# Two regroupings in a 14-stage transformer kernel: value products among the heads, and turned copies ahead of other work

## The chip, the cores and the metric

The kernel runs on one core of one Trainium2 chip. The time is the device time of one execution in microseconds (us), the median of the runs shown. A core has a matrix engine (TensorE, called PE in the rows; its weight loads are PEld), VectorE (DVE), ScalarE (ACT), GpSimd (POOL) and SyncE (SP), which issues most of the DMAs. The engines run their own lists of instructions in program order and wait for one another by counting semaphores.

## The reference, cut to what matters

Two transformer blocks run one after the other on 512 tokens of width 1024; the weights are float32. The change touches the hybrid mixer of the first block, the key and value products of the memory (256 rows) for its cross attention, and the sparse attention of the second block.

```python
def hybrid_mixer(hn, ...):
    z = hn @ w_in
    y_a = gmlp_spatial_gating(za[..., :D_A], za[..., D_A:], ln_a_g, ln_a_b, w_s, b_s)
    y_b = conformer_conv(zb[..., :D_B], zb[..., D_B:], conv_b_w, conv_b_b, gn_b_g, gn_b_b)
    y_c = mlstm_group(...)                       # 4 heads of 128
    return jnp.concatenate([y_a, y_b, y_c], axis=-1) @ w_out

def cross_attention(hn, mn, w_xq, w_xkv, w_xo):
    kv = mn @ w_xkv                              # mn = rmsnorm(mem): 256 x 1024
    k = kv[..., :D_MODEL].reshape(Bsz, M, N_XHEADS, DH_X)
    v = kv[..., D_MODEL:].reshape(Bsz, M, N_XHEADS, DH_X)
...
# second block, sparse attention, for each block of queries:
        p_s = masked_softmax(s_s, (kpos <= t[:, None])[:, :, None])
        o_s = jnp.einsum('bghqn,bgqnd->bghqd', p_s.astype(v_sel.dtype), v_sel)
```

## The kernel before, in words

**Number format.** Every float32 matrix product is made of three products: a rounded high part and the rest of each operand are held apart (`x_hi`, `x_lo`, `w_hi`, `w_lo`), and `hi*hi`, `hi*lo`, `lo*hi` are added up in PSUM. Small products (the gates, the heads, the attention) use plain float32.

**Weight tiles.** All weights come as one stream of 309 tiles of 128x1024, in the order in which `weight_stream` writes them, through a ring of four slots. SP loads tile t into `raw` when tile t-4 has been split. POOL splits it (L2389 writes `w_hi`, L2391 writes `w_lo`), and may start when PE has finished tile t-4 (`tile_done`). PE waits for `weights_split`, and for `tile_out`, which counts results taken out of PSUM by ACT or DVE. Tiles 0 to 16 are the mixer's input product, 17 to 32 the memory's keys and values (`mem_kv`: eight key tiles, then eight value tiles), 33 to 40 the mixer's output product (`mix_out`).

**PSUM.** There are eight banks of 512 columns: `acc` 0 to 3 and `misc` 0 to 3.

**The mixer on PE.** After the input product PE runs, by hand-written order: `cell_in(0)` (projections of head 0), `mem_k(0)` (one key tile: 24 products of 256 columns), `conv_mean` (two means of the convolution branch), `gating` (two products of the spatial gate, L651 and L655), `cell_scores(0)`, `mem_k(1)`, `cell_out(0)`. Then each of heads 1 to 3 is `cell_in`, `mem_k`, `cell_scores`, `mem_k`, `cell_turn` (transposes of the head before), `cell_out`. Then come the eight value tiles `mem_v(half, j)`: each half of the value's columns takes four tiles, 12 products of 512 columns each, into `acc` 0 and 1, and the second half waits until ACT has drained the first. `conv_var` and `cell_turn(3)` lie between them. Then `opening_of` runs the first three tiles of `mix_out` chunk by chunk (72 products of 512 columns), each chunk when ACT has written `y_hi` and DVE `y_lo` for it. `y_hi` and `y_lo` share memory with `mn_hi` and `mn_lo`, the normed memory, so ACT writes no `y_hi` until all of `mem_kv` is done.

**What the gate waits for.** `gating` needs `v_tok`, the normed tokens of the gate: DVE centres the convolution branch (L1896, which needs `conv_mean`), then does L1901, L1906 and L1909, four operations of 128x256 each. `cell_out(0)` waits for DVE's products of the gate (L1916).

**The memory norm.** Its sum of squares is one PE product after the first opening; ACT and DVE then write `mn_hi` and `mn_lo` chunk by chunk (`rms_high`, `rms`). DVE's convolution of the mLSTM branch (L1834, L1835) starts when five input tiles are out.

**Sparse attention.** There are 14 batches b. For each, PE makes scores (`n_scores`, L910, L914), DVE takes the maximum (`n_max`, L2207), ACT the exponential (`n_exp`, L1484), DVE the scaling (`n_scale`, L2217 to L2222). PE turns the probabilities (`n_turn`, L926) into `misc` 0 and 1; ACT copies the one to `pt_n` (L1515), DVE the other (L2246); PE multiplies them by the values (`n_values`, L941, L947). Scores run three batches ahead, values one behind.

## Time and profile before

| | before |
|---|---|
| median of 3 runs | 1947.76 us (1945.41 to 1947.98) |
| profiled execution | 1947.59 us, its span 1945.8 us |
| PE busy | 1892.9 us (97%) |
| DVE, ACT, POOL busy | 793.7, 432.0, 1071.2 us |
| mean granted TensorE clock | 0.991 |
| products on PE | 8938 |

The span runs from the first to the last instruction; 1.8 us of the profiled execution lie outside it. Matmuls overlap in the records, so the distance from one start to the next is the cost of a product, not its duration. A granted clock of 1.00 is TensorE's upper level of 2.4 GHz, and 0.50 is its lower level of 1.2 GHz.

### The profile page before, as it was taken

The page shows a single profiled execution, that of the slowest core. Times are in us where ns is not written, and L with a number is a line of the kernel's source. Part 1 is how long each engine was busy: PE and PEld are TensorE (multiplying, and loading weights), DVE is VectorE, ACT ScalarE, POOL GpSimd, SP SyncE. Part 2 cuts the span into 40 slices and gives each one's busy share as a digit, 9 for nine tenths or more (in the row PEclk, how much of TensorE's full clock was granted, in tenths as well). Part 3 has the DMA queues.
Part 4 walks back from the last instruction along what each step waited for, and adds up shares of the span by engine and source line. Part 5 has one row for each costly group of instructions (what it writes and reads, how often), then busy time and mean ns, then how long its engine had stood idle before and what let it go on. Part 6 is the DMA issues. An engine that isn't in the chain of part 4 may idle for free.

```text
span 1945.8 us, 24354 instructions
## 1 busy us (share of the span) xinstructions
PE 1892.9 (97%) x8938; PEld 1516.6 (78%) x8938; DVE 793.7 (41%) x1305; ACT 432.0 (22%) x850; POOL 1071.2 (55%) x622
## 2 busy tenths in 40 slices
PE   7989999999999999999999999999999999999997
PEld 5868787888888888875778888887776778888885
DVE  4965333343342434579451212136523371212126
ACT  4323322310000121045140101023414140101022
POOL 5734663565757656430456665564752446666552
PEclk9989999999999999999999999999999999999998
DMA  5322332222333325210123332222321223332321
GB/s 220 109 65 74 96 102 65 78 96 87 119 98 108 98 84 208 67 55 2 56 76 107 98 97 87 87 95 79 108 87 42 67 75 99 106 99 97 97 87 44
DMA packets 46879, 175.99 MB, mean 90 GB/s; under 512 B 5200, under 2 KB 5328, under 8 KB 46032
## 3 DMA queue, kind: packets, MB, share of 16 engines
q1 hardware_dynamic: 46512, 169.55, 27.0%
q10 hardware_dynamic: 288, 5.31, 0.7%
q8 instruction: 59, 0.97, 0.2%
q14 instruction: 20, 0.16, 0.0%
HBM read 172.74 MB, written 2.10 MB: 90 GB/s over the span
## 4 chain that ended last, share of the span: by engine, by line
PE 94%; DVE 3%; ACT 1%; issue 1%; POOL 0%; DMA 0%; SPq 0%; DVEq 0%; POOLq 0%
PE acc L471 17%; PE acc L473 17%; PE acc L472 17%; PE acc L498 7%; PE acc L494 7%; PE acc L495 7%; PE acc L521 1%; PE acc L522 1%; PE acc L523 1%; PE acc L1052 1%; PE misc L926 1%; PE acc L1054 1%; PE acc L1053 1%; PE acc L542 1%; PE acc L541 1%; PE acc L540 1%
## 5 line engine op out<-in xcount | busy, mean ns | idle before, releaser
L2389 POOL TENSOR_SCALAR w_hi<-raw 128x1024 fp32r<-128x1024 f32 x309 | 331.3, 1072 | 816.8 <-PE acc L498 323.3
L2391 POOL TENSOR_TENSOR w_lo<-raw,w_hi 128x1024 fp32r<-128x1024 f32 x309 | 744.7, 2410 | 25.8
L471 PE MATMUL acc<-x_hi,w_hi 128*128 128x512 f32 x872 | 343.3, 394 | 0.0
L473 PE MATMUL acc<-x_hi,w_lo 128*128 128x512 f32 x872 | 339.6, 389 | 0.0
L472 PE MATMUL acc<-x_lo,w_hi 128*128 128x512 f32 x872 | 339.4, 389 | 0.0
L1790 DVE TENSOR_TENSOR h<-acc,h 128x512 f32<-128x512 f32 x120 | 82.9, 691 | 367.7 <-PE acc L473 234.1
L471 PE MATMUL acc<-y_hi,w_hi 128*128 128x512 f32 x590 | 231.1, 392 | 0.0
L473 PE MATMUL acc<-y_hi,w_lo 128*128 128x512 f32 x590 | 229.6, 389 | 0.0
L472 PE MATMUL acc<-y_lo,w_hi 128*128 128x512 f32 x590 | 229.6, 389 | 0.0
L471 PEld LDWEIGHTS acc<-x_hi,w_hi 128*128 128x128 f32 x872 | 163.8, 188 | 35.4 <-issue 2.3
L473 PEld LDWEIGHTS acc<-x_hi,w_lo 128*128 128x128 f32 x872 | 163.7, 188 | 34.2
L472 PEld LDWEIGHTS acc<-x_lo,w_hi 128*128 128x128 f32 x872 | 163.9, 188 | 32.4
L1530 ACT ACTIVATE z<-acc 128x512 f32<-128x512 f32 x64 | 38.2, 598 | 463.0 <-PE acc L498 351.8
L494 PE MATMUL acc<-y_hi,w_hi 128*128 128x512 f32 x330 | 129.8, 393 | 4.2 <-ACT y_hi L1390 2.9
L2266 DVE TENSOR_TENSOR acc<-acc,z 128x512 f32<-128x512 f32 x64 | 44.6, 697 | 213.0 <-ACT z L1530 213.0
L472 PEld LDWEIGHTS acc<-y_lo,w_hi 128*128 128x128 f32 x590 | 110.7, 188 | 23.9 <-issue 1.0
L471 PEld LDWEIGHTS acc<-y_hi,w_hi 128*128 128x128 f32 x590 | 110.7, 188 | 23.8 <-issue 1.0
L495 PE MATMUL acc<-y_hi,w_lo 128*128 128x512 f32 x330 | 129.0, 391 | 0.0
L473 PEld LDWEIGHTS acc<-y_hi,w_lo 128*128 128x128 f32 x590 | 110.8, 188 | 22.9
L494 PE MATMUL acc<-x_hi,w_hi 128*128 128x512 f32 x240 | 93.7, 391 | 4.5 <-POOL w_lo L2391 2.7
L498 PE MATMUL acc<-y_lo,w_hi 128*128 128x512 f32 x330 | 93.5, 392 | 1.4 <-DVE y_lo L2372 1.4
L495 PE MATMUL acc<-x_hi,w_lo 128*128 128x512 f32 x240 | 93.4, 389 | 0.0
(398 smaller groups left out, 2650.2 us busy)
## 6 DMA issues: line engine op xcount, KB each, us to landing
raw<-weights_dram SPq DMA_DIRECT2D x309, 512.0 KB, 3.5
w_cmp<-w_cmp_dram ACTq DMA_DIRECT2D x1, 4096.0 KB, 14.7
h<-x_dram SPq DMA_DIRECT2D x2, 1024.0 KB, 6.5
out_dram<-h SPq DMA_DIRECT2D x8, 256.0 KB, 2.0
small<-small_dram SPq DMA_DIRECT2D x1, 1408.0 KB, 16.4
small<-small_dram ACTq DMA_DIRECT2D x1, 1088.0 KB, 5.0
mem_in<-mem_dram SPq DMA_DIRECT2D x1, 1024.0 KB, 13.5
const<-const_dram SPq DMA_DIRECT2D x1, 640.0 KB, 9.5
```

The costliest lines, as they stand in the source:

```text
L471: mm(out, m["w_hi"][:, slot, k], hi[:, k], start=k == 0, stop=False)
L472: mm(out, m["w_hi"][:, slot, k], lo[:, k], start=False, stop=False)
L473: last = mm(out, m["w_lo"][:, slot, k], hi[:, k], start=False, stop=k == kc - 1)
L494: mm(acc[:, slot], m["w_hi"][:, slot, k], hi[:, k], start=k == 0, stop=False)
L495: mm(acc[:, slot], m["w_lo"][:, slot, k], hi[:, k], start=False, stop=False)
L498: last = mm(acc[:, slot], m["w_hi"][:, slot, k], lo[:, k], start=False, stop=k == kc - 1)
L521: mm(out, hi[:, k, blk(b)], w_hi[:, blk(i, width)], start=k == 0 and first, stop=False)
L1530: f(z[:, slot], acc[:, slot], ACT.Relu).then_inc(sem(name + "_relu"), 1)
L1790: v.tensor_tensor(h[:, c], acc[:, slot], h[:, c], ALU.add).then_inc(sem("tile_out"), 1)
L2266: v.tensor_tensor(acc[:, slot], acc[:, slot], z[:, slot], ALU.mult).then_inc(sem(name + "_product"), 1)
L2389: nc.gpsimd.tensor_scalar(hi, m["raw"][:, slot], 1.0, 0.0, ALU.mult, ALU.add).then_inc(sem("weights_high"), 1)
L2391: nc.gpsimd.tensor_tensor(m["w_lo"][:, slot].rearrange("p k n -> p (k n)"), m["raw"][:, slot], bf(hi), ALU.subtract).then_inc(sem("weights ...
```

## The change

The change has six parts.

- **Value tiles in quarters.** The eight value tiles now hold 256 columns each, two tiles to a quarter of the columns, and stand in the weight stream between the key tiles (`K_TILE`, `V_TILE`). A tile is 24 products of 256 columns. `mem_v(0)`, `mem_v(1)`, `mem_v(2)` run after `cell_out` of heads 0, 1, 2; five remain after head 3. Quarters 0 and 1 use bank `acc` 1, quarter 2 `acc` 0, quarter 3 `misc` 0, so no drain lies between them at the end. `cell_turn` always uses `acc` 3, and `cell_in` of heads 2 and 3 waits for `cell_y`.
- **Gate products amid the first head.** `conv_mean` runs before `mem_k(0)`, and `cell_scores(0)` before `gating`. On DVE the gate's two products lie between the operations of head 0.
- **First two chunks of the output product apart.** The gate's result has its own `ya_hi` and `ya_lo`, which can be written before `mem_kv` ends; `mix_out` reads them for chunks 0 and 1. The opening no longer waits for all of `mem_kv` to be drained, only for 12 of its 16 results.
- **Memory norm sooner.** PE's sum of squares lies inside the first opening, before chunk 6. ACT writes four chunks of `mn_hi` before and four after the first three input results.
- **mLSTM convolution in pairs.** Its first two channels start when three input results are out.
- **Sparse attention.** In batch 0 ACT and DVE copy the turned probabilities before `n_exp(2)`, and before `n_max(2)` and `pool_low(1)`. On PE `n_values(0)` comes before `n_scores(4)`.

```diff
@@ -64,6 +64,13 @@
 HALF = KC // 2
 
 
+K_TILE = [0, 1, 3, 4, 6, 7, 9, 10]
+V_TILE = [2, 5, 8, 11, 12, 13, 14, 15]
+
+K_OUT = [1, 2, 3, 4, 7, 8, 9, 10]
+V_OUT = [6, 12, 14, 16]
+
...
@@ -337,6 +348,8 @@
                  ("v_stats", [TB, 6]), ("v_mv", [TB, 2]), ("v_rstd", [TB]), ("g_col", [TB, 4]), ("em_col", [TB, 4]),
                  ("cell_r", [TB]), ("cell_s", [TB])])
     assert e <= end, (e, end)
+    place("ya_hi", [2, S], F32R, e - 4 * (TB * 256 + 2 * S + 2 * (CONV_B - 1) + TB * 6 + TB * 2 + 3 * TB + 2 * TB * 4))
+    place("ya_lo", [2, S], F32R, e - 4 * (TB * 256 + TB * 6 + TB * 2 + 3 * TB + 2 * TB * 4))
...
+            if free is None:
+                claim(t0 + j)
+            else:
+                pe.wait_ge(sem("weights_split"), t0 + j + 1)
+                pe.wait_ge(sem("tile_out"), free)
         for k in range(kc):
             if also:
...
+    def memory_norm(k):
+        if k == 6:
+            pe.wait_ge(sem("norm_rstd"), 1)
+            sum_squares("mem", MEM)
+
+    opening(0, 0, "mix", memory_norm)
...
-        t = START["mem_kv"] + c
+        t = START["mem_kv"] + K_TILE[c]
         pe.wait_ge(sem("weights_split"), t + 1)
-        pe.wait_ge(sem("tile_out"), t)
+        pe.wait_ge(sem("tile_out"), START["mem_kv"] + (K_OUT[c - 1] if c else 0))
...
-    def mem_v(half, j):
-
-        t = START["mem_kv"] + 8 + 4 * half + j
+    def mem_v(j):
+
+        t = START["mem_kv"] + V_TILE[j]
         pe.wait_ge(sem("weights_split"), t + 1)
-        if j == 0:
-            pe.wait_ge(sem("tile_out"), t)
...
+        if j == 2:
+            pe.wait_ge(sem("tile_out"), START["mem_kv"] + V_OUT[0])
+        if j == 4:
+            pe.wait_ge(sem("tile_out"), START["mem_kv"] + K_OUT[7])
+        if j == 6:
+            pe.wait_ge(sem("std_scaled"), 1)
+        bank = pr.values_bank(j // 2)
...
+            out = bank[:, blk(b, 256)]
+            for i in range(4):
+                k = 4 * (j % 2) + i
+                w_hi, w_lo = (m[w][:, t % RING].rearrange("p k n -> p (k n)")[:, blk(i, 256)] for w in ("w_hi", "w_lo"))
+                mm(out, m["mn_hi"][:, k, blk(b)], w_hi, start=k == 0 and b == 0, stop=False)
+                mm(out, m["mn_hi"][:, k, blk(b)], w_lo, start=False, stop=False)
+                last = mm(out, m["mn_lo"][:, k, blk(b)], w_hi, start=False, stop=k == KC - 1 and b == 1)
...
+        if head >= 2:
+            pe.wait_ge(sem("cell_y"), head - 1)
...
-            last = turn(acc[:, 1 if head < 3 else 3, blk(tb)], m["cell_tok"][:, tb], ident)
+            last = turn(acc[:, 3, blk(tb)], m["cell_tok"][:, tb], ident)
...
     pe.wait_ge(sem("tile_out"), START["mem_kv"])
     pe.wait_ge(sem("row_cols_out"), 2)
     cell_in(0)
+    for c in range(2):
+        conv_mean(c)
     pe.wait_ge(sem("norm_ready"), chunks_before("mem") + KC)
     mem_k(0)
-    for c in range(2):
-        conv_mean(c)
+    cell_scores(0)
     for c in range(2):
         gating(c)
-    cell_scores(0)
     mem_k(1)
     cell_out(0)
+    mem_v(0)
     for head in range(1, 4):
...
         cell_turn(head - 1)
         cell_out(head)
-    mem_v(0, 0)
-    mem_v(0, 1)
+        if head < 3:
+            mem_v(head)
+    mem_v(3)
+    mem_v(4)
     for c in range(2):
         conv_var(c)
-    mem_v(0, 2)
+    mem_v(5)
     cell_turn(3)
-    mem_v(0, 3)
-    for j in range(4):
-        mem_v(1, j)
+    mem_v(6)
+    mem_v(7)
     pe.wait_ge(sem("cell_y"), 4)
-    pe.wait_ge(sem("tile_out"), END["mem_kv"])
-
-
-    opening_of(START["mix_out"], START["mix_out"], y_hi, y_lo, "y_high", "y_ready", 0)
+
+
+    mix_hi, mix_lo = Parts(m["ya_hi"], 2, y_hi), Parts(m["ya_lo"], 2, y_lo)
+    opening_of(START["mix_out"], START["mix_out"], mix_hi, mix_lo, "y_high", "y_ready", 0, free=START["mem_kv"] + 12)
     for c in range(3, KC):
-        dense(START["mix_out"] + c, (START["mix_out"] + c) % RING, y_hi, y_lo)
+        dense(START["mix_out"] + c, (START["mix_out"] + c) % RING, mix_hi, mix_lo)
...
     for b in range(len(BATCHES)):
         n_turn(b)
+        if b == 1:
+            n_values(0)
         if b + 3 < len(BATCHES):
             n_scores(b + 3)
-        if b:
+        if b > 1:
             n_values(b - 1)
...
+    rms_high("mem", m["mn_hi"], MEM, range(4))
...
-    rms_high("mem", m["mn_hi"], MEM)
...
+    rms_high("mem", m["mn_hi"], MEM, range(4, KC))
...
+        out(START["mem_kv"] + K_TILE[c], 0, m["mem_k"][:, c], src=acc[:, 0, 0:MEM])
+
+    def mem_v(quarter):
+        act.wait_ge(sem("tile_done"), START["mem_kv"] + V_TILE[2 * quarter + 1] + 1)
+        f(m["mem_v"][:, :, blk(quarter, 256)], pr.values_bank(quarter).rearrange("p (b n) -> p b n", b=2), ACT.Copy)\
+            .then_inc(sem("tile_out"), 2)
...
+        if head == 1:
+            mem_v(0)
     cell_root(3)
+    act.wait_ge(sem("y_a"), 2)
+    for c in range(2):
+        f(m["ya_hi"][:, c], m["y_mix"][:, c], ACT.Copy).then_inc(sem("y_high"), 1)
     for c in range(2):
...
         rsqrt(misc[:, c, :], misc[:, c, :], 1.0, LN_EPS, "std_rstd")
+    mem_v(1)
     cell_gain(3)
-    mem_v(0)
     for c in range(2):
         act.wait_ge(sem("std_scaled"), c + 1)
         f(m["conv_b"][:, c], m["conv_b"][:, c], ACT.Silu, scale=pr.col("gn_b_g", c), bias=pr.col("gn_b_b", c))\
             .then_inc(sem("y_b"), 1)
-    mem_v(1)
     act.wait_ge(sem("tile_done"), END["mem_kv"])
-    act.wait_ge(sem("y_a"), 2)
     act.wait_ge(sem("y_b"), 2)
-    for c in range(KC):
+    for c in range(2, KC):
         if c >= 4:
             act.wait_ge(sem("cell_y"), c - 3)
         f(m["y_hi"][:, c], m["y_mix"][:, c], ACT.Copy).then_inc(sem("y_high"), 1)
+    mem_v(2)
+    mem_v(3)
 
     residual_rms("xat", START["mix_out"], "norm_x_g")
 
...
         tb, br, c0, heads = BATCHES[b]
         n = heads * (tb + 1) * P
-        if b + 2 < len(BATCHES):
+        if b and b + 2 < len(BATCHES):
             n_exp(b + 2)
         act.wait_ge(sem("n_turned"), 2 * b + 1)
         if b >= 2:
             act.wait_ge(sem("n_values"), b - 1)
         f(m["pt_n"][:, b % 2, 0, 0:n], misc[:, 0, 0:n], ACT.Copy).then_inc(sem("n_pt0"), 1)
+        if b == 0:
+            n_exp(2)
         if b and BATCHES[b - 1][0] < tb:
             n_high(tb - 1)
     for g in (2, 3):
...
-    dve.wait_ge(sem("tile_out"), 5)
     dve.wait_ge(sem("norm_high"), 2 * KC)
...
+    for pair in range(2):
+        dve.wait_ge(sem("tile_out"), 3 + 2 * pair)
+        before = own.n
...
-    dve.wait_ge(sem("tile_out"), START["mem_kv"])
-    for c in range(2):
+    def gate(c):
         dve.wait_ge(sem("gating"), c + 1)
         v.tensor_tensor(m["u_a"][:, c], m["u_a"][:, c], misc[:, 2 + c, :], ALU.mult).then_inc(sem("y_a"), 1)
...
         v.tensor_tensor(m["y_mix"][:, 4 + head], bank, m["oc_gate"][:, head], ALU.mult).then_inc(sem("cell_y"), 1)
 
     cell_diagonal(0)
+    dve.wait_ge(sem("tile_out"), START["mem_kv"])
+    gate(0)
     cell_weights(0)
+    gate(1)
     cell_norm(0)
     for head in range(1, 4):
         cell_weights(head)
         cell_final(head - 1)
         cell_norm(head)
     for c in range(2):
+        dve.wait_ge(sem("y_high"), c + 1)
+        v.tensor_tensor(m["ya_lo"][:, c], m["y_mix"][:, c], bf(m["ya_hi"][:, c]), ALU.subtract).then_inc(sem("y_ready"), 1)
+    for c in range(2):
         dve.wait_ge(sem("std_rstd"), c + 1)
         v.tensor_tensor(m["conv_b"][:, c], m["conv_b"][:, c], misc[:, c, :], ALU.mult).then_inc(sem("std_scaled"), 1)
     cell_final(3)
-    for c in range(KC):
+    for c in range(2, KC):
...
     v.tensor_copy(m["pct"][:, 4:8], misc[:, 2, :].rearrange("p (j n) -> p j n", j=4)).then_inc(sem("cmp_pt"), 1)
     n_scale(1)
-    n_max(2)
-    pool_low(1)
     pool_order = [(g, k) for g in (2, 3) for k in range(g + 4)]
     for b in range(len(BATCHES)):
         tb, br, c0, heads = BATCHES[b]
@@ -2244,7 +2304,10 @@
         if b >= 2:
             dve.wait_ge(sem("n_values"), b - 1)
         v.tensor_copy(m["pt_n"][:, b % 2, 1, 0:n], misc[:, 1, 0:n]).then_inc(sem("n_pt1"), 1)
-        if 0 < b < len(BATCHES) - 1:
+        if b == 0:
+            n_max(2)
+            pool_low(1)
+        elif b < len(BATCHES) - 1:
             n_scale(b + 1)
         if b + 3 < len(BATCHES):
             n_max(b + 3)

```

The same pattern (chunks 0 and 1 apart, four channels as two pairs) repeats in the lines left out; `Parts` is a small class that picks `ya` for chunks 0 and 1 and `y` for the rest, and `values_bank` holds the banks named above.

On PE around the gate, before; `y_mix,const` is `conv_mean`, `small_64` rows that write `misc` are `gating`, `q_c,k_c` rows are `cell_scores(0)`, `mn` rows belong to a key tile:

```order
L619 MATMUL acc<-mn_hi,w_lo 128x256
L641 MATMUL misc<-y_mix,const 128x512 x2
L651 MATMUL misc<-small_64,const 128x512
L655 MATMUL misc<-small_64,v_tok 64x128 x8
L651 MATMUL misc<-small_64,const 128x512
L655 MATMUL misc<-small_64,v_tok 64x128 x8
L677 MATMUL misc<-q_c,k_c 128x512
L677 MATMUL misc<-q_c,k_c 128x384
L677 MATMUL misc<-q_c,k_c 128x128
L677 MATMUL acc<-q_c,k_c 128x256
L617 MATMUL acc<-mn_hi,w_hi 128x256
```

The same place now, first the start and then the end of the key tile of 24 products:

```order
L710 MATMUL acc<-small_64,xc 128x128 x4
L680 MATMUL misc<-y_mix,const 128x512 x2
L652 MATMUL acc<-mn_hi,w_hi 128x256
L653 MATMUL acc<-mn_lo,w_hi 128x256
L654 MATMUL acc<-mn_hi,w_lo 128x256
```

```order
L654 MATMUL acc<-mn_hi,w_lo 128x256
L718 MATMUL misc<-q_c,k_c 128x512
L718 MATMUL misc<-q_c,k_c 128x384
L718 MATMUL misc<-q_c,k_c 128x128
L718 MATMUL acc<-q_c,k_c 128x256
L690 MATMUL misc<-small_64,const 128x512
L694 MATMUL misc<-small_64,v_tok 64x128 x8
L690 MATMUL misc<-small_64,const 128x512
L694 MATMUL misc<-small_64,v_tok 64x128 x8
L652 MATMUL acc<-mn_hi,w_hi 128x256
```

The means moved ahead of the key tile, and key tile and scores now both lie between them and the gate.

On ACT at the end of the mixer, before (`y_hi<-y_mix` are the high parts for the output product):

```order
L1353 ACTIVATE acc<-acc,par 128x512
L1182 ACTIVATE mem_v<-acc 128x512
L1344 ACTIVATE mem_v<-acc 128x512
L1381 ACT_TABLE_LOAD
L1381 ACTIVATE y_mix<-y_mix,par 128x512 x2
L1182 ACTIVATE mem_v<-acc 128x512
L1344 ACTIVATE mem_v<-acc 128x512
L1390 ACTIVATE y_hi<-y_mix 128x512 x8
```

and now:

```order
L1425 ACTIVATE ya_hi<-y_mix 128x512 x2
L1231 ACTIVATE misc<-misc 128x512
L1232 ACTIVATE misc<-misc 128x512
L1231 ACTIVATE misc<-misc 128x512
L1232 ACTIVATE misc<-misc 128x512
L1390 ACTIVATE mem_v<-acc 128x2x256
L1400 ACTIVATE acc<-acc,par 128x512
L1433 ACT_TABLE_LOAD
L1433 ACTIVATE y_mix<-y_mix,par 128x512 x2
L1440 ACTIVATE y_hi<-y_mix 128x512 x6
L1390 ACTIVATE mem_v<-acc 128x2x256
L1390 ACTIVATE mem_v<-misc 128x2x256
```

Two high parts moved ahead of the value tiles' end, and two drains moved behind the other six.

On DVE in the sparse attention, before, from the scaling of batch 1 on (`n_neg` is a maximum, `pt_n` the copy of turned probabilities):

```order
L2222 TENSOR_SCALAR p_n<-p_n,n_r 128x128 x8
L2207 TENSOR_REDUCE n_neg<-acc 128x2x2
L2198 SCALAR_TENSOR_TENSOR y_lo<-misc,par,y_hi 128x512
L2246 COPY pt_n<-misc 128x512
L2207 TENSOR_REDUCE n_neg<-acc 128x2x2
L2130 TENSOR_TENSOR pool_s<-u_n 128x527
L2246 COPY pt_n<-misc 128x512
```

and now:

```order
L2284 TENSOR_SCALAR p_n<-p_n,n_r 128x128 x8
L2306 COPY pt_n<-misc 128x512
L2269 TENSOR_REDUCE n_neg<-acc 128x2x2
L2260 SCALAR_TENSOR_TENSOR y_lo<-misc,par,y_hi 128x512
L2269 TENSOR_REDUCE n_neg<-acc 128x2x2
L2192 TENSOR_TENSOR pool_s<-u_n 128x527
L2306 COPY pt_n<-misc 128x512
```

The first copy moved ahead of one maximum and one low part.

## Rows read from the trace of the kernel before

**Rows 1.** Page, chain that ended last: share of the span by engine.
```profile
PE 94%; DVE 3%; ACT 1%; issue 1%; POOL 0%; DMA 0%; SPq 0%; DVEq 0%; POOLq 0%
```

**Rows 2.** Waits of PE, whole span: waiter, releaser, total us, times, longest us.
```profile
PE misc L651 <- DVE v_tok L1909: 5.9, 1, 5.9
...
PE acc L634 <- ACT mem_v L1344: 1.3, 1, 1.3
```

**Rows 3.** Timeline of PE around the gate: start, us, instruction, [idle before, releaser].
```profile
119.88 0.36 PE L617 MATMUL acc<-mn_hi,w_hi 128*128 128x256 f32 x1
...
122.83 1.88 PE L641 MATMUL misc<-y_mix,const 128*128 128x512 f32 x4
130.57 2.04 PE L651 MATMUL misc<-small,const 2*128 2x512 f32 x2 [5.86 <-DVE v_tok L1909]
...
138.36 3.78 PE L677 MATMUL misc<-q_c,k_c 128*128 128x512 f32 x6
...
142.22 0.47 PE L617 MATMUL acc<-mn_hi,w_hi 128*128 128x256 f32 x1
```

**Rows 4.** Timeline of PE in head 1: scores, and the key tile behind.
```profile
154.24 1.89 PE L677 MATMUL misc<-q_c,k_c 128*128 128x512 f32 x6
...
156.21 0.47 PE L617 MATMUL acc<-mn_hi,w_hi 128*128 128x256 f32 x1
```

**Rows 5.** Windows: stretch, its us, busy us of PE, PEld, DVE, ACT, POOL, PEclk, DMA.
```profile
128.25:142.00 13.75, 11.43 (x43) 6.15 (x44) 5.43 (x15) 1.08 (x4) 0.00 (x0) 0.50 0.09 33
220.50:224.00 3.50, 3.50 (x10) 2.72 (x9) 3.50 (x3) 2.57 (x4) 2.68 (x1) 0.51 0.35 133
858.75:865.60 6.85, 5.28 (x28) 3.94 (x30) 4.88 (x11) 3.90 (x16) 0.00 (x0) 0.50 0.01 2
...
868.23:890.54 22.31, 21.80 (x182) 12.85 (x183) 21.61 (x55) 12.21 (x37) 0.00 (x0) 1.00 0.00 1
```

**Rows 6.** Timeline of DVE ahead of the gate.
```profile
125.35 2.43 DVE L1901 TENSOR_SCALAR v_tok<-v_tok,v_mv,v_rstd 128x256 f32<-128x256 f32 x4
...
129.05 1.42 DVE L1909 TENSOR_TENSOR v_tok<-v_tok,small 128x256 f32<-128x256 f32 x4
```

**Rows 7.** Timeline of POOL: splits at the gate and before the output product.
```profile
124.32 2.35 POOL L2391 TENSOR_TENSOR w_lo<-raw,w_hi 128x1024 fp32r<-128x1024 f32 x1
...
212.06 1.05 POOL L2389 TENSOR_SCALAR w_hi<-raw 128x1024 fp32r<-128x1024 f32 x1
...
215.55 1.05 POOL L2389 TENSOR_SCALAR w_hi<-raw 128x1024 fp32r<-128x1024 f32 x1
```

**Rows 8.** Timeline of PE: 20 products of a key tile, 42 of value tiles.
```profile
120.32 0.28 PE L617 MATMUL acc<-mn_hi,w_hi 128*128 128x256 f32 x1
...
122.71 0.28 PE L619 MATMUL acc<-mn_hi,w_lo 128*128 128x256 f32 x1
...
206.13 0.39 PE L634 MATMUL acc<-w_hi,mn_hi 128*128 128x512 f32 x1
...
215.68 0.39 PE L634 MATMUL acc<-w_hi,mn_hi 128*128 128x512 f32 x1
```

**Rows 9.** Timeline of PE: opening of the output product, and its next tile.
```profile
219.38 0.47 PE L494 MATMUL acc<-y_hi,w_hi 128*128 128x512 f32 x1 [2.87 <-ACT y_hi L1390]
...
237.40 0.39 PE L471 MATMUL acc<-y_hi,w_hi 128*128 128x512 f32 x1
```

**Rows 10.** Timeline of PE, ACT and DVE in the sparse attention.
```profile
860.32 1.97 PE L926 MATMUL misc<-const,p_n 128*128 128x128 f32 x8 [3.59 <-ACT pt_n L1515]
...
867.05 1.09 PE L926 MATMUL misc<-const,p_n 128*128 128x128 f32 x8
...
859.66 0.60 ACT L1515 ACTIVATE pt_n<-misc 128x512 f32<-128x512 f32 x1
...
862.39 0.69 DVE L2246 COPY pt_n<-misc 128x512 f32<-128x512 f32 x1 [1.58 <-PE misc L926]
...
868.23 0.69 DVE L2246 COPY pt_n<-misc 128x512 f32<-128x512 f32 x1 [1.53 <-PE misc L926]
```

76 lines of the change are left out of this document (36 added, 40 removed).

## The prediction

> **What bounds the kernel now.** I read the chain that ended last first: PE carries 94% of it [rows 1], so time is won only where PE stands still or runs slowly. The waits of PE and its timeline in the two places of the change come next. In the mixer PE waits 5.9 us for `v_tok` and 1.3 us for a drain of the values [rows 2], and 2.87 us for the first `y_hi` of the output product [rows 9]. In the sparse attention it waits 3.59 us for a copy of turned probabilities [rows 10]. Last I read the windows for the granted clock: behind the three longer waits TensorE stands at its lower level of 1.2 GHz, from 128.25 to 142, from 220.5 to 224 and from 858.75 to 865.6 us [rows 5]. No such stretch follows the wait of 1.3 us. So each long wait costs twice, once as idle time and once as half speed behind it.
>
> **The gate, part by part.** Before, PE needs 142.22 - 119.88 = 22.3 us from the start of `mem_k(0)` to that of `mem_k(1)` [rows 3]. The same work now starts with `conv_mean` at about 119.9. PE then has the means (row of 1.88, some 1.8 net of overlap), the key tile (122.83 - 119.88 = 2.95) and the scores (156.21 - 154.24 = 1.97 at full clock [rows 4]): 6.7 us of cover. DVE's way from the means to `v_tok` took 130.57 - 122.83 = 7.7 us [rows 3]. Within it L1901 took 2.43 us. POOL's subtraction ran until 124.32 + 2.35 = 126.67, and L1901's four operations ended 1.1 us after that, at 127.78 [rows 6, 7]. So about 1.3 us of the 7.7 was a wait for POOL. POOL's next split now starts when the key tile ends, some 4.8 us behind the means, and DVE is by then in its last eight operations (L1906, L1909; 1.42 us per four [rows 6]). I take 7.7 - 1.3 = 6.4 us, under the cover of 6.7, so PE does not wait. The bounds are a wait of 0 and, if POOL's 1.05 and 2.35 both get in front of DVE, 6.4 + 3.4 - 6.7 = 3.1 us. Without a wait the clock stays up. The gate's products, 138.36 - 130.57 = 7.8 us at half clock, then take 3.9, and the scores 1.97 instead of 142.22 - 138.36 = 3.86. Saved: 5.9 + 3.9 + 1.9 = **11.7 us**.
>
> The Trainium skill (SBUF — State Buffer, Who interferes with whom) says that a VectorE instruction with two SBUF inputs and a GpSimd instruction that reads SBUF exclude each other, and that the one issued first goes first. By that rule L1906 and L1909, with two SBUF inputs each, hold POOL off if they come first, and the sum stays as it is; if POOL is first, it is the rival of the port below. That L1901 ended 1.1 us after POOL's subtraction agrees with it.
>
> **Value tiles.** Before, they are 96 products of 512 columns at 9.55 / 42 = 0.227 us [rows 8], 21.8 us. Now they are 192 of 256 columns at 2.39 / 20 = 0.1195 us [rows 8], 22.9 us. That costs 1.1 us, or 1.8 if every tile costs the 2.95 of a lone key tile. Three of eight stand alone, so I take **1.2 us**. The Trainium skill (TensorE: Matmul & The Clock Gate, Back-to-back issue gap) gives columns / 2.4 GHz + 2.5 ns for the warm gap; by it the split would cost 96 x 2.5 ns = 0.2 us, and the forecast would be 1 us lower. The rows decide. The drain between the halves is gone: **1.3 us** saved [rows 2]. Now ACT drains quarter 0 ahead of the exponentials of head 2. That hides behind `cell_in(2)`, whose first product the exponentials need anyway. `cell_in` of heads 2 and 3 waits for `cell_y`, but a value tile of 2.9 us stands in between, which hides DVE's last operation. Should that cover be gone, each such wait costs under 1 us.
>
> **The opening of the output product.** Before, PE waits 2.87 us there, because no `y_hi` may be written until the value tiles end [rows 9]. Chunks 0 and 1 are now ready long before. Chunk 2 needs one ACT and one DVE operation behind the last value tile, 1.3 us by their kind, while chunks 0 and 1 give PE 18 x 0.227 = 4.1 us. Next late is POOL. Tile 34 can be split only when value tile 5 is done, tile 35 follows it, and the opening needs both: two splits at 215.55 - 212.06 = 3.49 us each [rows 7], 7.0 us. PE has a turn (0.4 us, my estimate) and two value tiles, 2 x 24 x 0.1195 = 5.7 us, in that time. So 0.9 us is left, with 0.3 of start lag 1.2. DVE's two `ya_lo` subtractions may hold POOL up a little more. I take a saving of **1.5 us** (0 to 2.9). The opening itself ran 237.40 - 219.38 = 18.0 us [rows 9], where 72 products at 0.227 are 16.4. With a wait as short as the 1.3 us that left the clock alone, that is **1.6 us** saved.
>
> **Edits at nothing.** The memory norm's sum is the same one product in another place; its input has been ready for over a microsecond when chunk 6 is reached, and ACT and DVE have slack between the first opening and the third input tile. The mLSTM convolution in pairs starts and ends sooner, but DVE then waits for input tiles 7 and 8, so the long convolution of the other branch ends as before, and PE reaches `conv_mean` no earlier than 119.9 anyway. If it ended over 1.4 us later the gate would be late by the excess. The DMAs and their order on SP stay the same; only what a tile holds is changed.
>
> Mixer: 11.7 - 1.2 + 1.3 + 1.5 + 1.6 = **14.9 us**.
>
> **Sparse attention.** PE stood idle 3.59 us from 856.7 and worked 865.6 - 860.32 = 5.3 us at half clock, which lost 2.6. So 6.2 us is the upper bound. The copy of batch 0 on ACT, at 859.66 [rows 10], stood behind `n_exp(2)`, which waited for DVE's maximum. It can now run as soon as the turn is done, before PE's wait even began. Next late are `n_exp(2)`, pushed back by DVE's copy (0.7 us by its kind), and the copy of batch 1 behind `n_exp(3)`. By these PE reaches the third turn near 862.7 instead of 867.05, 4.3 us sooner. But DVE sets the pace behind it: it is busy 21.61 of 22.31 us from 868.23 on [rows 5], so only DVE's own lead lasts. Its two waits for PE, 1.58 and 1.53 us [rows 10], go, and some tenths where it waited for scores: 3.1 to 3.7. I take **3.5 us** (0 to 6.2). No instruction is added there.
>
> Sum: 14.9 + 3.5 = 18.4 us from the profiled execution of 1947.59 us, which is as good as the median of 1947.76: **1929.2 us**.
>
> **The rivals.**
>
> *The clock falls in the gate.* Work resumed at 130.57, but the clock rose only at 142, 11.4 us later and 3.6 us into the scores; in the other two stretches it rose 4.6 and 5.3 us after work resumed [rows 5, 9, 10]. So the gate's small products (2 rows, or 64 columns) do not lift the clock, and they may let it fall. It would then be down for about 4.6 to 5.3 us of key tile and `cell_out`, a loss of 2.5 us: 1931.7. Against it: the products last 3.9 us only, with dense work on both sides.
>
> *The port goes to POOL.* PE waits 3.1 us, longer than the 2.87 that cost the clock before, and gate and scores' successors run at half speed again, another 5 to 6 us: 1938.
>
> *The sparse part gives nothing.* The copy goes first, but `n_exp(2)` and `n_max(2)` are pushed back by it, and DVE's pace swallows the rest: 18.4 - 3.5 saved, 1932.7. For it: DVE's 97%. Against it: DVE did wait twice for PE.
>
> *Slower: the clock stays down through the heads.* If the gate lets it fall and the heads' mix of small products, now with value tiles among them, does not lift it, PE runs at half speed for three heads. From one head's second key tile to the next's it took 156.21 - 142.22 = 14.0 us [rows 3, 4], with a value tile 16.9, so some 50 us would be lost and 1979 be the result. It decides from 18.4 us of full-speed work done at half clock on. Against it: head 1 ran at full clock before with the same small products [rows 4], and a value tile is dense.
>
> **How the numbers follow.** The forecast has 0.60, the clock in the gate 0.17, the sparse part 0.10, the port 0.08, the slower case 0.02, and 0.03 is left for the unforeseen. The forecast's own spread is 1926.5 to 1931.5 (waits at the opening, DVE's lead). A range of 1926.0 to 1934.5 takes in the first three cases and little of the fourth, somewhat over 0.8. A measurement here can tell about 0.2%, or 3.9 us, from no change; every case but the slower one and part of the unforeseen is faster by more: faster 0.94, same 0.03, slower 0.03.
>
> **What the profile would show.** Right: no wait of PE at the gate over 1 us; clock 1.00 from 120 to 210; opening near 206 instead of 219.38, with a wait of 1 to 1.5 us released by POOL and a length of 16.4 us; second turn in the sparse attention without the 3.59 us, clock at 1.00 there, third turn 4 us nearer to the first. Wrong: a clock of 0.50 behind the gate, an L1965 (the old L1909) stretched by POOL, `n_scores(4)` waiting long for `n_exp(2)`, or PE waits in the heads that were not there.

## The result, and the profile after

| | before | after |
|---|---|---|
| median of 3 runs | 1947.76 us (1945.41 to 1947.98) | 1932.98 us (1932.86 to 1933.06) |
| profiled execution, its span | 1947.59, 1945.8 us | 1933.06, 1931.3 us |
| mean granted TensorE clock | 0.991 | 0.995 |
| products on PE, busy | 8938, 1892.9 us | 9034, 1888.9 us |

The ratio of the mean times is 0.9928, with a 95% interval of 0.9915 to 0.9941: faster, by 14.5 us of span, where 18.4 us were forecast. The time lies in the range given (1926.0 to 1934.5), 3.8 us above its likeliest value and outside the forecast's own spread (1926.5 to 1931.5).

Waits of PE over the whole span, after (waiter, releaser, total us, times, longest us). The 5.9 us for `v_tok` and the 1.3 us for the drain [rows 2] are gone. What is left in the mixer is the `w_lo` line: of its two waits the longer one, 2.1 us, is the one ahead of the output product; the other is at the kernel's start.

```profile
PE acc L526 <- POOL w_lo L2454: 3.7, 2, 2.1
```

Timeline of PE at the gate, after (start, us, instruction), rows that answer to [rows 3]: the means, the first, second and fourth of the four rows of the gate's products, the start of the key tile `mem_k(1)`, and the output of head 0.

```profile
119.77 1.88 PE L680 MATMUL misc<-y_mix,const 128*128 128x512 f32 x4
...
126.61 1.12 PE L690 MATMUL misc<-small,const 2*128 2x512 f32 x2
127.66 1.09 PE L694 MATMUL misc<-small,v_tok 128*64 128x128 f32 x16
...
129.74 1.59 PE L694 MATMUL misc<-small,v_tok 128*64 128x128 f32 x16
131.25 0.58 PE L652 MATMUL acc<-mn_hi,w_hi 128*128 128x256 f32 x1
...
135.25 2.39 PE L735 MATMUL misc<-v_c,p_c 128*128 128x129 f32 x20
```

No wait stands among them. But the fourth row of the gate took 1.59 us where the second took 1.09, and the key tile took 135.25 - 131.25 = 4.0 us instead of 2.95. The windows say why (columns as in [rows 5]: stretch, its us, busy us of PE, PEld, DVE, ACT, POOL, then the granted clock and the DMA): the clock was at its lower level behind the gate, and once more in the output product's opening. The third window, in the sparse attention, shows the upper level throughout.

```profile
130.20:133.40 3.20, 3.20 (x22) 2.87 (x19) 1.65 (x4) 0.00 (x0) 0.00 (x0) 0.50 0.53 164
208.70:212.10 3.40, 3.40 (x10) 2.66 (x9) 3.40 (x2) 2.85 (x5) 3.20 (x2) 0.50 0.54 159
...
854.00:876.00 22.00, 20.73 (x173) 12.06 (x170) 21.31 (x55) 13.32 (x43) 0.00 (x0) 1.00 0.00 1
```

On DVE the way from the means to `v_tok` now ends at 124.93 + 1.42 = 126.35, 0.26 us before PE asks for it. POOL's split began amid it and was held up, not DVE: its `w_hi` took 2.54 us instead of 1.05 (L1965 is the old L1909; the old L1901 now took 1.38 us instead of 2.43). All eleven experiments show the same at this place, 2.53 or 2.54 us. First DVE, then POOL:

```profile
124.93 1.42 DVE L1965 TENSOR_TENSOR v_tok<-v_tok,small 128x256 f32<-128x256 f32 x4
```

```profile
124.72 2.54 POOL L2452 TENSOR_SCALAR w_hi<-raw 128x1024 fp32r<-128x1024 f32 x1 [5.70 <-PE acc L654]
```

The opening of the output product on PE, and the next tile behind it, the rows that answer to [rows 9]:

```profile
208.11 0.47 PE L526 MATMUL acc<-ya_hi,w_hi 128*128 128x512 f32 x1 [2.07 <-POOL w_lo L2454]
...
226.20 0.40 PE L499 MATMUL acc<-ya_hi,w_hi 128*128 128x512 f32 x1
```

The wait is 2.07 us, and the opening is 226.20 - 208.11 = 18.1 us long, as before. Ahead of it POOL worked without a gap on four tiles. Of them these rows show the first tile's `w_lo`, which is the long one, and the last tile's. The row below is DVE's, which began 0.06 us after the long one:

```profile
193.71 3.56 POOL L2454 TENSOR_TENSOR w_lo<-raw,w_hi 128x1024 fp32r<-128x1024 f32 x1
...
205.38 2.37 POOL L2454 TENSOR_TENSOR w_lo<-raw,w_hi 128x1024 fp32r<-128x1024 f32 x1
```

```profile
193.77 1.28 DVE L2048 TENSOR_TENSOR ya_lo<-y_mix,ya_hi 128x512 fp32r<-128x512 f32 x2
```

The sparse attention on PE, the first, second, third and sixth turn (the second is two rows), to lay beside [rows 10]:

```profile
843.23 1.04 PE L969 MATMUL misc<-const,p_n 128*128 128x128 f32 x8
...
845.50 0.60 PE L969 MATMUL misc<-const,p_n 128*128 128x128 f32 x4
846.27 0.66 PE L969 MATMUL misc<-const,p_n 128*128 128x128 f32 x4 [0.17 <-DVE pt_n L2306]
...
851.67 1.10 PE L969 MATMUL misc<-const,p_n 128*128 128x128 f32 x8 [0.85 <-ACT pt_n L1567]
...
863.17 1.13 PE L969 MATMUL misc<-const,p_n 128*128 128x128 f32 x8
```

Three rows of the kernel before are needed for the ledger and stand in no group ahead: `cell_in(1)`, and the first and the sixth turn.

```profile
147.61 1.12 PE L663 MATMUL acc<-row_M,const 4*128 4x512 f32 x2
...
854.30 1.04 PE L926 MATMUL misc<-const,p_n 128*128 128x128 f32 x8
...
877.70 1.12 PE L926 MATMUL misc<-const,p_n 128*128 128x128 f32 x8
```

**The ledger**, forecast against the two traces:

| term | forecast | measured | from |
|---|---|---|---|
| gate, up to `mem_k(1)` | 11.7 | 10.9 | 22.3 - (131.25 - 119.77) |
| `mem_k(1)` and `cell_out(0)` | 0 | -0.8 | 147.61 - 142.22 = 5.4 before; 137.40 - 131.25 = 6.15 now |
| value tiles and drain | +0.1 | +0.3 | the rest of the mixer |
| wait ahead of the opening | 1.5 | 0.8 | 2.87 - 2.07 |
| length of the opening | 1.6 | -0.1 | 18.0 - 18.1 |
| mixer (with 0.1 of an earlier start) | 14.9 | 11.2 | 237.40 - 226.20 |
| sparse attention | 3.5 | 3.5 | (877.70 - 854.30) - (863.17 - 843.23) |

The first value tile starts at 137.40. Some 0.1 us is lost between the two places, and the sum is 14.5 us. So two places carry the miss: 1.6 us at the gate, and 2.4 us at the output product.

### The profile page after: what moved, and what is told of

Read it like the earlier page. It is cut to its first block, busy times and chain, and to the rows that moved or that the text cites. A ratio compares the mean times of both kernels' runs of the same rounds, so it can differ in the third digit from the quotient of the medians.

```text
span 1931.3 us, 24553 instructions
## 1 busy us (share of the span) xinstructions
PE 1888.9 (98%) x9034; PEld 1518.7 (79%) x9034; DVE 791.8 (41%) x1305; ACT 431.6 (22%) x850; POOL 1075.5 (56%) x622
## 4 chain that ended last, share of the span: by engine, by line
PE 94%; DVE 3%; issue 1%; POOL 1%; ACT 1%; DMA 0%; SPq 0%; DVEq 0%; POOLq 0%
PE acc L499 17%; PE acc L501 17%; PE acc L500 17%; PE acc L530 7%; PE acc L526 7%; PE acc L527 7%; PE acc L553 1%; PE acc L555 1%; PE acc L554 1%; PE acc L1097 1%; PE acc L1099 1%; PE acc L1098 1%; PE acc L573 1%; PE acc L574 1%; PE acc L572 1%; PE misc L806 1%
## 5 line engine op out<-in xcount | busy, mean ns | idle before, releaser
L499 PE MATMUL acc<-y_hi,w_hi 128*128 128x512 f32 x580 | 227.3, 392 | 0.0
L501 PE MATMUL acc<-y_hi,w_lo 128*128 128x512 f32 x580 | 225.7, 389 | 0.0
L500 PE MATMUL acc<-y_lo,w_hi 128*128 128x512 f32 x580 | 225.7, 389 | 0.0
L526 PE MATMUL acc<-y_hi,w_hi 128*128 128x512 f32 x324 | 126.8, 391 | 1.3 <-ACT y_hi L1699 1.3
L527 PE MATMUL acc<-y_hi,w_lo 128*128 128x512 f32 x324 | 126.1, 389 | 0.0
L530 PE MATMUL acc<-y_lo,w_hi 128*128 128x512 f32 x324 | 91.2, 389 | 1.4 <-DVE y_lo L2435 1.4
```

The source lines that it names most:

```text
L499: mm(out, m["w_hi"][:, slot, k], hi[:, k], start=k == 0, stop=False)
L500: mm(out, m["w_hi"][:, slot, k], lo[:, k], start=False, stop=False)
L501: last = mm(out, m["w_lo"][:, slot, k], hi[:, k], start=False, stop=k == kc - 1)
L526: mm(acc[:, slot], m["w_hi"][:, slot, k], hi[:, k], start=k == 0, stop=False)
L527: mm(acc[:, slot], m["w_lo"][:, slot, k], hi[:, k], start=False, stop=False)
L530: last = mm(acc[:, slot], m["w_hi"][:, slot, k], lo[:, k], start=False, stop=k == kc - 1)
```

## The experiments

Each kernel was timed in turns with the kernel before, whose medians were 1947.19, 1947.29 and 1947.50 us in the three sittings. An execution's time varies more here than the medians suggest, and the reason turned out to be the main finding, so the single times are given. "The changed kernel" is the one above.

### The low parts of chunks 0 and 1, moved out of POOL's way

```diff
@@ ACT, behind mem_k(1) of head 0 (was: behind cell_root(3)) @@
+    act.wait_ge(sem("y_a"), 2)
+    for c in range(2):
+        f(m["ya_hi"][:, c], m["y_mix"][:, c], ACT.Copy).then_inc(sem("y_high"), 1)
@@ DVE, behind cell_norm(0) (was: behind cell_norm(3)) @@
+    for c in range(2):
+        dve.wait_ge(sem("y_high"), c + 1)
+        v.tensor_tensor(m["ya_lo"][:, c], m["y_mix"][:, c], bf(m["ya_hi"][:, c]), ALU.subtract).then_inc(sem("y_ready"), 1)
```

> The changed kernel with the high and low parts of chunks 0 and 1 of the output product written amid head 0 and 1 instead of behind head 3; the rest is as it is. In the changed kernel VectorE's two subtractions of these low parts ran from 193.77 for 1.28 us, and GpSimd's w_lo at 193.71 took 3.56 us instead of the 2.39 of its neighbours, at the head of a row of four tiles without a gap that ends at 207.75 and releases the output product at 208.11. Theory (the subtractions held GpSimd up): that w_lo takes 2.4 us, the four tiles end 1.2 us sooner, and the wait of TensorE falls from 2.07 to 0.9 us. If a wait so short leaves the clock alone, as one of 1.3 us did before, the opening's 72 products take 16.4 instead of 18.1 us: 1.2 + 1.7 = 2.9 us faster than the changed kernel, about 1930.1 us. Rival 1: the clock falls all the same, since what comes before the wait or the length of it doesn't decide: 1.2 us faster, 1931.8. Rival 2: the w_lo was long for another reason: no change, 1933.0.

Measured: 1929.11 us (1930.85, 1929.06, 1929.13, 1929.08), ratio to the kernel before 0.9907 (0.9892 to 0.9922). In the profiled execution, that of 1930.85, POOL's split at this place and the opening read:

```profile
193.77 2.38 POOL L2454 TENSOR_TENSOR w_lo<-raw,w_hi 128x1024 fp32r<-128x1024 f32 x1
...
200.12 1.04 POOL L2452 TENSOR_SCALAR w_hi<-raw 128x1024 fp32r<-128x1024 f32 x1 [0.47 <-PE acc L675]
...
204.76 2.37 POOL L2454 TENSOR_TENSOR w_lo<-raw,w_hi 128x1024 fp32r<-128x1024 f32 x1
```

```profile
207.48 0.46 PE L526 MATMUL acc<-ya_hi,w_hi 128*128 128x512 f32 x1 [1.38 <-ACT y_hi L1440]
...
224.02 0.40 PE L499 MATMUL acc<-ya_hi,w_hi 128*128 128x512 f32 x1
```

The `w_lo` is 1.2 us shorter. The wait names ACT as its releaser, but ACT had been writing high parts since 206.14, and the wait ended 0.35 us after POOL's last split (204.76 + 2.37 = 207.13): it is POOL still. It fell to 1.38 us and not to 0.9, because POOL then waited 0.47 us for the end of a value tile before tile 34, which is the forecast's own picture: two splits of 3.5 us behind value tile 5, with a wait of 1.2 forecast. The opening took 224.02 - 207.48 = 16.5 us. With POOL out of the way both terms of the opening come out nearly as forecast. At the gate the clock did fall in this execution (its fourth row took 1.98 us), which is 1.5 us and fits the other three times, 1929.06 to 1929.13.

### Two products of full size in the wait

```diff
     mem_v(7)
+    pe.wait_ge(sem("tile_out"), START["mem_kv"] + 12)
+    idle_products(2, 1)
     pe.wait_ge(sem("cell_y"), 4)
```

> The changed kernel with two products of 512 columns into bank acc 1, whose results nobody reads, between the last value tile and the output product, where TensorE waits 2.07 us for GpSimd. Two such products take about 1.8 us (0.96 us from one start to the next of the like in the first head). The end of the wait is set by GpSimd and stays. Theory (the idle time lets the clock fall behind it, from 208.7 to 212.1 at its lower level): the clock stays at 1.00 and the opening takes 16.4 instead of 18.1 us, 1.7 us faster than the changed kernel, 1931.3. Rival: the clock falls for another reason, such as what stands before the wait: the same 18.1 us and 1933.0, or up to 0.3 later if the products outlast the wait.

Measured: 1930.04 us (1929.53, 1930.04, 1929.92, 1932.49, 1931.81), ratio 0.9917 (0.9903 to 0.9931). The median is 1.3 us below the expected 1931.3, and two of the five times are above it. The opening of the profiled execution started at 206.19 without a wait, with the clock at 1.00 (row below), and was 16.5 us long. But two other things differed in this trace. First, the clock had not fallen at the gate, whose code is that of the changed kernel: the fourth row of the gate and the key tile are at full speed.

```profile
206.00:212.00 6.00, 6.00 (x26) 4.79 (x26) 6.00 (x6) 4.08 (x7) 4.01 (x2) 1.00 0.45 115
```

```profile
119.81 1.88 PE L680 MATMUL misc<-y_mix,const 128*128 128x512 f32 x4
...
129.78 1.09 PE L694 MATMUL misc<-small,v_tok 128*64 128x128 f32 x16
130.81 0.39 PE L652 MATMUL acc<-mn_hi,w_hi 128*128 128x256 f32 x1
...
135.92 0.36 PE L673 MATMUL acc<-w_hi,mn_hi 128*128 128x256 f32 x1
```

Second, DVE's subtraction was held up this time and not POOL. It started 0.06 us behind POOL's `w_lo`, exactly as in the changed kernel, with the opposite outcome (first POOL, then DVE):

```profile
192.23 2.38 POOL L2456 TENSOR_TENSOR w_lo<-raw,w_hi 128x1024 fp32r<-128x1024 f32 x1
```

```profile
192.29 2.86 DVE L2050 TENSOR_TENSOR ya_lo<-y_mix,ya_hi 128x512 fp32r<-128x512 f32 x1
```

The Trainium skill (SBUF — State Buffer, Who interferes with whom) says that a VectorE instruction with two SBUF inputs and a GpSimd instruction that reads SBUF exclude each other. The traces agree: in the changed kernel POOL's `w_lo` took 1.2 us more, and here DVE's first subtraction took 2.2 us more. Here it went on behind that: the two subtractions took 4.30 us together instead of 1.28, and the next tile's split, beside the second of them, took 1.49 and 2.71 us instead of 1.04 and 2.39. It also says that the first to issue has the ports; by the start times alone POOL was first in both, and once it was held up and once not, so the recorded starts do not tell who will be.

So this run agrees with the theory but doesn't prove it. It was the first sign that the clock at the gate is not the same in every execution.

### The gate's products on either side of the key tile

```diff
-    for c in range(2):
-        gating(c)
-    mem_k(1)
+    gating(0)
+    mem_k(1)
+    gating(1)
@@ cell_out(0) @@
-            pe.wait_ge(sem("y_a"), 2)
+            pe.wait_ge(sem("y_a"), 1)
...
+            if head == 0 and tb == 2:
+                pe.wait_ge(sem("y_a"), 2)
```

> The changed kernel with the key tile mem_k(1) between the two gate products instead of behind both; cell_out(0) waits for the second product of VectorE's gate only before its third block. In the changed kernel scores and gate are 6.9 us in a row without a dense tile, and the clock stood at its lower level from 130.2 to 133.4, which cost about 1.4 us. Theory (the gate's products of two rows and of 64 columns, 4.6 us in a row, let the clock fall): with half of them on either side of a dense tile it stays at 1.00, and the output of the head starts 1.4 us sooner, less up to 0.8 us that it may wait for the gate's second product: 0.6 to 1.4 us faster, 1931.6 to 1932.4. Rival: the clock falls behind the first half already, or behind the second, in front of cell_out(0): no gain, 1933.0, or some tenths slower.

Measured: 1931.36 us (1931.83, 1929.95, 1929.74, 1931.36, 1931.54), ratio 0.9915 (0.9901 to 0.9928). In the profile the clock stayed up through the gate, and fell behind the wait of 2.06 us ahead of the output product (windows, columns as above):

```profile
126.50:137.00 10.50, 10.50 (x88) 8.39 (x88) 4.46 (x14) 1.47 (x5) 6.42 (x4) 1.00 0.23 59
207.90:211.20 3.30, 3.30 (x9) 2.62 (x8) 3.30 (x3) 2.40 (x4) 2.72 (x2) 0.50 0.37 142
```

From `cell_in(0)` to the first value tile it took 20.26 us, against 21.40 in the changed kernel's trace and 19.87 in the one above, where the clock had stayed up as well. The split thus costs 0.4 us and may save 1.5. The times don't show a gain by themselves: the median, 1931.36, is that of the changed kernel when it was timed again below (1931.50), but two of the five executions are below 1930, and none of the changed kernel's eight is.

### The change without its sparse part

```diff
@@ ACT @@
-        if b and b + 2 < len(BATCHES):
+        if b + 2 < len(BATCHES):
             n_exp(b + 2)
...
-        if b == 0:
-            n_exp(2)
@@ DVE, and on PE n_values(0) behind n_scores(4) as before @@
     n_scale(1)
+    n_max(2)
+    pool_low(1)
...
-        if b == 0:
-            n_max(2)
-            pool_low(1)
-        elif b < len(BATCHES) - 1:
+        if 0 < b < len(BATCHES) - 1:
```

> The changed kernel without its part in the sparse attention: the first copies of turned probabilities stand again behind the exponentials and the maximum, and the values of batch 0 behind the scores of batch 4. By the two traces this part gave 14.52 - 11.07 = 3.45 us. Theory (it stands on its own and VectorE's pace keeps 3.45 of the 6.2 us): 3.4 to 3.5 us slower than the changed kernel, 1936.4, with the wait of 3.59 us and the lower clock back. Rival (part of the difference came from elsewhere, or is given back in the stage behind): under 2.5 us slower.

Measured: 1935.65 us (1935.65, 1936.22, 1935.09, 1935.25, 1936.71), ratio 0.9941 (0.9928 to 0.9955). The wait of 3.6 us was back. The clock fell only 0.8 us after work had resumed, and stood lower for 3.4 us of work. Before the change it had fallen during the wait and stood lower for 6.85 us, 5.3 of them work [rows 5, 10]:

```profile
850.05:853.45 3.40, 3.40 (x19) 2.05 (x19) 2.36 (x8) 1.56 (x7) 0.00 (x0) 0.50 0.00 0
```

```profile
843.26 1.04 PE L969 MATMUL misc<-const,p_n 128*128 128x128 f32 x8
...
849.28 1.30 PE L969 MATMUL misc<-const,p_n 128*128 128x128 f32 x8 [3.60 <-ACT pt_n L1565]
...
865.75 1.12 PE L969 MATMUL misc<-const,p_n 128*128 128x128 f32 x8
```

From the first to the sixth turn it took 865.75 - 843.26 = 22.5 us, against 23.4 before the change and 19.9 after it. So the part is worth 2.55 or 3.46 us, by how long the clock stays down in the version without it. The run with the gate alone, below, has the old order here too, and there it also took 22.5 us. The medians (1935.65 here, 1931.50 for the changed kernel below) hold other falls of the clock too and can't tell the two apart. The part stands alone; the 3.5 us were one of two sizes, and the one that two of the three profiles of the old order show is the smaller, between the expected 3.45 and the rival's 2.5.

### The changed kernel once more

> The changed kernel once more, without an edit, beside the others. The same code at the gate had the clock at its lower level for 3.2 us in three profiles (the changed kernel and two of its variants) and at 1.00 in a fourth, and the five times of that variant lie in two groups some 2 us apart. Theory (whether the clock falls at the gate varies from execution to execution): the times lie again in two groups 1.5 to 2 us apart, at about 1933.0 and 1931.3 us, and so the 1.5 us at the gate are lost only in part of the executions. Rival (in the changed kernel it falls always): all at 1932.9 to 1933.1.

Measured: 1931.50 us (1933.05, 1931.52, 1931.30, 1931.31, 1931.50), ratio 0.9919 (0.9905 to 0.9932). Two groups, as the theory has it; with the three runs above the changed kernel has eight times, four from 1931.30 to 1931.52 and four from 1932.86 to 1933.06. The profile, of 1933.05, has no fall at the gate, and the fall in the opening. Its other 1.5 us came before all of this: `cell_in(0)` started at 117.51 instead of 116.00. The cause is a third fall of the clock, at the kernel's start. PE reaches the first opening behind a wait for the first weight tiles, 3.22 us here and 1.66 in the changed kernel's first trace. The weights weren't late: the opening began at 20.57 here and at 20.64 there. The wait was longer because the products ahead of it ran at full speed sooner (PE, this run):

```profile
14.61 1.02 PE L595 MATMUL misc<-sum_sq,const 128*128 128x512 f32 x2
...
20.57 0.47 PE L526 MATMUL acc<-x_hi,w_hi 128*128 128x512 f32 x1 [3.22 <-POOL w_lo L2454]
```

and the same rows in the first trace of the changed kernel:

```profile
14.94 1.91 PE L595 MATMUL misc<-sum_sq,const 128*128 128x512 f32 x2
...
20.64 0.47 PE L526 MATMUL acc<-x_hi,w_hi 128*128 128x512 f32 x1 [1.66 <-POOL w_lo L2454]
```

Behind the wait of this run the clock stood at its lower level, which the first trace doesn't have (window, columns as above):

```profile
21.20:24.60 3.40, 3.40 (x10) 2.66 (x9) 3.40 (x6) 1.55 (x3) 2.52 (x2) 0.50 0.98 392
```

So each of the two profiled executions, 1933.06 and 1933.05, had two falls, the one at the gate and in the opening, the other at the start and in the opening.

### The gate alone

```diff
@@ the kernel before, PE @@
-    pe.wait_ge(sem("norm_ready"), chunks_before("mem") + KC)
-    mem_k(0)
     for c in range(2):
         conv_mean(c)
+    pe.wait_ge(sem("norm_ready"), chunks_before("mem") + KC)
+    mem_k(0)
+    cell_scores(0)
     for c in range(2):
         gating(c)
-    cell_scores(0)
@@ DVE @@
     cell_diagonal(0)
+    dve.wait_ge(sem("tile_out"), START["mem_kv"])
+    gate(0)
     cell_weights(0)
+    gate(1)
```

> The kernel before with one part of the change, the gate: on TensorE the means ahead of mem_k(0) and the scores ahead of the gate's products, on VectorE the gate's two products between the operations of head 0. Value tiles, output product, memory norm, convolution and sparse attention are as before. Forecast: this part is 11.7 us; by the trace of the changed kernel 10.86 us up to mem_k(1), less 0.76 behind it, 10.1 us. Theory (it stands alone, and the clock falls in it or not): 10.1 to 11.6 us faster than the kernel before, 1937.6 to 1936.0 us, with no wait of TensorE at the gate. Rival (it needs the other edits, such as the convolution in pairs, so that VectorE's way is short enough): a wait of over 1 us for v_tok and the lower clock behind it, under 8 us faster, above 1939.

Measured: 1935.30 us (1935.49, 1935.11, 1933.68, 1937.00), ratio 0.9938 (0.9923 to 0.9954), 12.0 us by the medians. That is 0.4 us beyond the expected 10.1 to 11.6. No wait stood at the gate, so it needs none of the other edits: neither the memory norm's nor the convolution's new place. The clock fell there (first window), which cost the same 1.5 us. The row of PE is a surprise: the wait ahead of the output product is the old 2.87 us, and the clock did not fall behind it (second window), so that the opening took 226.21 - 209.76 = 16.5 us.

```profile
130.45:133.60 3.15, 3.15 (x23) 2.82 (x22) 1.81 (x5) 0.00 (x0) 0.00 (x0) 0.52 0.54 166
209.76:214.00 4.24, 4.24 (x19) 3.49 (x20) 4.24 (x3) 3.69 (x6) 3.82 (x2) 1.00 0.41 124
```

```profile
137.99 1.12 PE L663 MATMUL acc<-row_M,const 4*128 4x512 f32 x2
...
209.76 0.47 PE L494 MATMUL acc<-y_hi,w_hi 128*128 128x512 f32 x1 [2.87 <-ACT y_hi L1390]
```

So the 12.0 us are not all the gate's. From `cell_in(0)` to `cell_in(1)` it took 137.99 - 116.42 = 21.57 us, against 147.61 - 116.20 = 31.41 before: 9.8 us, with a fall in it. The other two places are unchanged code, and there the clock was kinder than in the trace before: 1.5 us in the opening, and 0.9 in the sparse attention (22.5 us instead of 23.4, the clock lower for 3.4 us behind the same wait of 3.59). Less 0.2 us of a later start, these make up the 12.0.

### More small products, and more full ones, behind the gate

```diff
@@ the first of the two, between gating and mem_k(1) @@
+    for _ in range(4):
+        mm(acc[:, 1], half_sel[0:2], b_s[0:2, blk(0)].unsqueeze(1).to_broadcast([2, TB, P]), start=True, stop=True)
@@ the second, in the same place @@
+    idle_products(4, 1)
```

> The changed kernel with four more products of 2 rows and 512 columns, the kind of the gate's bias, into bank acc 1 behind the gate's own products; nobody reads them. At 1.05 us each they add 4.2 us to TensorE at full clock. Theory (products of so few rows count as little work, and the longer such a stretch the surer the fall): the clock is at its lower level through them and into mem_k(1), in every execution; they take up to 8.4 us and the key tile 4 to 6: 6 to 11 us slower than the changed kernel, 1939 to 1944. Rival (the rows don't matter, the fall at the gate comes from elsewhere): 4.2 us slower, 1937.2, and the clock as before.

Measured, small ones: 1939.88 us (1940.06, 1939.88, 1939.70, 1940.18, 1934.86), ratio 0.9956 (0.9943 to 0.9969). The clock fell soon after the added products began and stayed down for 10 us, through them (the row of eight, 5.8 us instead of 4.2) and the whole key tile behind:

```profile
133.95:144.10 10.15, 10.15 (x33) 7.08 (x32) 0.00 (x0) 0.30 (x1) 0.13 (x1) 0.50 0.04 16
```

```profile
132.51 5.84 PE L758 MATMUL acc<-small,const 2*128 2x512 f32 x8
138.28 0.58 PE L652 MATMUL acc<-mn_hi,w_hi 128*128 128x256 f32 x1
...
143.56 2.68 PE L735 MATMUL misc<-v_c,p_c 128*128 128x129 f32 x20
```

> The same place as in f3_small_filler, but four products of 128 rows and 512 columns (0.9 us each at full clock), so 3.6 us of TensorE added, and the gate's own products as they are. Theory (few rows let the clock fall): here it falls as in the changed kernel or less, since full products stand behind the gate; 3.6 us slower than the changed kernel at most, 1936.6 us, and less by up to 1.5 us if the fall is gone. Rival (the fall comes from the length of the time since the last dense tile, whatever the products' rows): as slow as f3_small_filler.

Measured, full ones: 1935.73 us (1936.76, 1935.11, 1936.35, 1934.91), ratio 0.9939 (0.9924 to 0.9955). In the profile the clock fell at 129.95, in the gate's own fourth row, and was up again 3.45 us later, still within the added products:

```profile
129.95:133.40 3.45, 3.45 (x19) 2.39 (x19) 2.08 (x5) 0.00 (x0) 0.00 (x0) 0.51 0.50 152
```

With nearly the same PE time added (4.2 and 3.6 us), the small products cost 8.4 us over the changed kernel's 1931.50 and the full ones 4.2. That is as expected of the rows, and the rival (as slow as the small ones) is out: the rows of a product count, and behind small ones the clock stayed down longer. "In every execution" was too strong. In one of five (1934.86) it seems to have stayed up: that execution's mean granted clock is 0.997, the others' 0.993 or 0.994. The profile of the small ones also has the fall at the kernel's start, behind a wait of 3.29 us, and its gate's own four rows ran at full speed. Behind the usual wait of 2.09 us ahead of the output product, the clock did not fall in the profile with the small products; with the full ones it did.

### The versions put together

> e1_early_lows and e3_gate_split together. The profiled run of e1_early_lows had its opening 16.5 us long behind a wait of 1.38 us, and its clock fell at the gate; e3_gate_split's stayed up at the gate and fell behind the 2.06 us in front of the output product. Theory (each edit keeps one of the two falls away in most executions): neither fall in the profile, and a median near 1929.5 us: the 1929.1 that three of four executions of e1_early_lows took, plus some 0.4 us that TensorE loses between the gate's halves by the two traces (20.26 against 19.87 us from cell_in(0) to mem_v(0) where neither fell); the highest of the times under 1930.5. Rival (the split does nothing for the clock, its executions only happened to be spared): times in two groups, at 1929.5 and 1931.

Measured: 1929.78 us (1931.18, 1929.47, 1929.73, 1929.82), ratio 0.9906 (0.9889 to 0.9922). In the profile, which is the execution of 1931.18, there is no fall at the gate or in the opening, as expected. It has the fall at the kernel's start, behind a wait of 2.93 us; its `cell_in(0)` starts at 117.57, and that is its 1.5 us.

```diff
@@ the next, on top of the early low parts @@
-    for c in range(2):
-        conv_var(c)
     mem_v(5)
+    for c in range(2):
+        conv_var(c)
     cell_turn(3)
@@ values_bank, quarter 3 @@
-self.misc[:, 0]
+self.misc[:, 2]
```

> e1_early_lows, and the two products conv_var one value tile later, behind mem_v(5); quarter 3 of the values goes to bank misc 2 instead of misc 0, so that nothing waits for them. In e1_early_lows GpSimd could start on tile 34 only at 200.12, when mem_v(5) was done, and two splits of 3.5 us followed, to 207.13; TensorE had 6.1 us in that time and waited 1.38. Theory (the wait is these two splits less what TensorE still has behind mem_v(5)): mem_v(5) ends 1.3 us sooner, tile 34 starts when GpSimd comes free at 199.65, the wait falls to 0.9 us and the kernel is 0.5 us faster than e1_early_lows, 1928.6 us where the clock stays up, 1930.1 where it falls at the gate. Rival (the later variance makes chunk 2 of the output product late, or GpSimd is held up by VectorE's scaling in its new place): the opening starts sooner but stops at its third chunk, 1929.1 or later.

Measured: 1930.58 us (1930.48, 1930.69, 1929.04, 1930.91), ratio 0.9908 (0.9892 to 0.9925). The wait was 1.19 us instead of 1.38, not 0.9: tile 34 was split from 199.51 on, as expected, but tile 35 only from 203.33 on, behind the end of value tile 6. The median, 1930.58, is above the expected 1928.6 to 1930.1. The clock fell at the gate and not at the opening.

```profile
207.20 0.46 PE L526 MATMUL acc<-ya_hi,w_hi 128*128 128x512 f32 x1 [1.19 <-ACT y_hi L1440]
```

> The edits of e1_early_lows, e3_gate_split and g2_early_var together. Theory (they add up): the wait in front of the output product 0.9 us, no fall of the clock at the gate or behind that wait, 0.5 us less than g1_early_split, a median near 1929.0 us with all times within 1 us. Rival (the split's 0.4 us is more than the falls that it keeps away): slower than g2_early_var at the median.

Measured: 1929.62 us (1929.80, 1930.89, 1929.44, 1929.36), ratio 0.9907 (0.9890 to 0.9923). There is no fall in the profile, but the median is 0.6 us above the expected 1929.0 and the times are 1.5 us apart instead of within 1. The four versions with early low parts are within 1.5 us of each other at the median, and their executions overlap, so none of them is shown to be the best. All of them beat the changed kernel: their 16 executions took 1929.04 to 1931.18 us, its eight 1931.30 to 1933.06.

## Why the prediction was right, and where it was not

**The clock over all profiles.** Counted over the thirteen profiles (before, after, eleven experiments): at the gate as the change has it, the clock fell in six of eight (not in the run with products in the wait and not in the repeat; the one with more small products is not counted); with the key tile between the halves in none of three. Ahead of the output product, with the wait of 2.1 us it fell in five of six; with 2.87 us in one of two; with 1.2 to 1.4 us in none of four; without a wait in none of one. At the kernel's start it fell behind waits of 2.93, 3.22 and 3.29 us and in none of the other ten, with 1.65 to 2.67 us. The counts are small, and the same code went either way.

**What goes with the draw.** The product of L595 at the start (L563 in the kernel before) shows how soon the clock rose in an execution, long before the gate. In three profiles it took 1.02 or 1.03 us; these are the three with the fall at the start, and the two of them whose gate can be compared (the repeat, and the one with more small products up to the end of the gate's own) had none there. In eight it took 1.91 or 1.92 us; of these the clock fell at the gate in all six without the split and in neither of the two with it. Of the remaining two, the run with products in the wait (1.46 us) had a fall in neither place, and the kernel before (1.28 us) has another gate. So the fall at the gate goes with something that is already settled in the first microseconds, and a lucky draw of this kind does not explain the two profiles with the split. This is read from counts; no experiment moved the moment of the rise.

**The gate: right.** The cover held, by 0.26 us; DVE took 126.35 - 119.77 = 6.6 us, where 6.4 was forecast against a cover of 6.7 (6.84 measured), and POOL's splits were the side that was held up, so the rival of the port fell. Where the clock stayed up, in the run with two products in the wait, the way from the means to `mem_k(1)` was 130.81 - 119.81 = 11.0 us and that to the value tile 5.1: a saving of 11.3 + 0.3 = 11.6 against a forecast of 11.7. The gate alone gave 9.8 us by its trace, with the fall in it, which is 1.5 us.

**The clock in the gate: the wrong case was taken.** The first rival came true in the profile of the changed kernel. Its price was 1.5 us, not the 2.5 that was forecast, since the clock fell near the end of the gate and was up after 3.2 us. Its chance of 0.17 was too low: it came in six profiles of eight. The step that failed is the argument against it, that the products last 3.9 us only with dense work on both sides. The rows that spoke for it had been read: before the change the clock stayed down through 7.8 us of the same products [rows 3, 5], where after other waits it rose within 4.6 and 5.3 us of work.

**The wait ahead of the opening: a size was off.** 0.8 us were saved where 1.5 were forecast. The working had the two splits right and put DVE's two subtractions down as "a little more". They cost POOL 1.2 us, and PE 0.7, as the first experiment showed: it took them away, and the wait came to 1.38 where 1.2 was forecast.

**The length of the opening: the term failed.** 1.6 us were counted because a wait of 1.2 would leave the clock alone. The wait was 2.07, and the clock fell. With waits of 1.2 to 1.4 us it never fell in four profiles, and the opening took 16.5 us. So the rule that the term took from before (1.3 us harmless, 2.87 not) held at its lower end, and the term fell with the wait. At its upper end it is no rule: behind the same 2.87 us the clock stayed up in the run with the gate alone.

**Value tiles and drain** were forecast as +0.1 us together and came to +0.3. **The edits at nothing** cost nothing that the ledger shows: `cell_in(0)` started at 116.00 instead of 116.20, and the gate worked without them.

**The sparse part: right, with a size that depends on the clock.** The second turn came without its wait, the third 4.3 us nearer to the first (12.75 before, 8.44 now), and DVE's pace kept 3.46 of that, all as forecast. But the 3.5 us were met because sum and ledger rest on the same profile before, in which the clock had its long fall. With the shorter one, as in the two other profiles of the old order, DVE's pace keeps 2.55.

**The total.** The forecast lacked 1.5 us at the gate, 0.7 at the wait and 1.7 in the opening. The first is a matter of execution to execution, the second is repaired by moving two subtractions, and the third mostly goes with the second: three of the four executions of the first experiment took 1929.1 us. That this is the forecast's 1929.2 is partly chance, since it is another kernel and the sparse part's size was a draw. That the measured time lies in the range is owed to the rivals for which it was widened: the first of them, 1931.7, is nearer to it than the forecast. What stays open is what sets the moment at which the clock first rises in an execution, and why the falls in the opening go either way.

## What to carry to other kernels

A half-clock stretch in one profile is a draw, not a constant: before its loss is put into a sum or credited to a change, give it with and without, and look at the spread of single execution times, which here came in steps of 1.5 to 2 us. When operations with two inputs in SBUF are put on VectorE beside a chain of GpSimd splits that ends in a release, the chain may pay for them (it did in six of seven profiles); look for a place where GpSimd is idle. Products of a few rows did not keep TensorE's clock up here in four of five executions, so a stretch of them that is moved between other small work is where to look for a fall; a dense tile between them costs 0.4 us here, and none of the three profiles with it showed the fall. And a longer wait in a trace need not mean that what is waited for came later: compare the times at which the waits end.

## What the runs showed of the hardware that was not expected

- The same instructions with the same wait went either way: behind 2.87 us of idle time the opening took 18.0 us in one profile and 16.5 in another.
- With the same wait of 3.6 us in the sparse attention the lower clock lasted 6.85 us in one profile and 3.4 us in two others.
- At the kernel's start the clock fell behind a wait of 2.93 us or more in three profiles and not behind one of 2.67 us or less in ten. The three waits were longer because the products ahead of them ran at full speed sooner, and each execution lost 1.5 to 1.6 us behind them.
- POOL's `w_lo` and DVE's subtraction, started 0.06 us apart in both cases, cost POOL 1.2 us in six of the seven profiles with the subtractions in this place. In the seventh the two subtractions cost DVE 3.0 us and POOL's next split 0.8.
- Through 4.2 us worth of added two-row products and behind them the clock stayed down for 10.15 us, the key tile of 24 full products included, which took 143.56 - 138.28 = 5.3 us instead of 2.95.
